# Splitting per-head sums, roots and VectorE's half of the output projection into plan steps of their own, in a two-layer backbone kernel on one core

## What is computed

```
h = modulate(rms_norm(x), shift1, scale1)
q_na, k_na, v_na, p, cq, ckv, krope = split(h @ w_in)     # 384 384 384 256 256 128 32 columns
q_na, k_na = rms_norm per head (6 heads of 64)
q_mla      = rms_norm per head(rms_norm(cq) @ w_uq)        # 6 heads of 96
k_mla, v   = from rms_norm(ckv) @ w_ukv and krope, k normed per head
o = concat(neighbourhood attention, pooling, latent attention)
x = x + gate1 * (o @ w_out)
h2 = modulate(rms_norm(x), shift2, scale2)
x = x + gate2 * peer(h2)   # 8 heads x 16 experts per token: rows u[e], v[e] of 1024 floats, gathered
```

## Time and profile before

| | us |
|---|---|
| three runs, median (lowest to highest) | 4258.71 (4248.27 to 4259.67) |
| the profiled execution's own time | 4255.55 |
| its span in the trace | 4253.7 |
| PE busy in it | 3637.2 (86%) |
| POOL busy | 2586.6 (61%) |
| DVE busy | 2550.2 (60%) |
| ACT busy | 963.9 (23%) |

### The profile page before, as it was taken

One profiled execution on the slowest core, in us unless ns is written; L12 is line 12 of the kernel. 1 busy time (PEld: TensorE's weight loads), 2 busy tenths in 40 slices (PEclk: granted clock), 3 DMA queues, 4 the chain that ended last, 5 costly groups with the idle time before them and its releaser, 6 DMA issues.

```text
span 4253.7 us, 37633 instructions
## 1 busy us (share of the span) xinstructions
PE 3637.2 (86%) x10554; PEld 1695.8 (40%) x10554; DVE 2550.2 (60%) x6442; ACT 963.9 (23%) x2490; POOL 2586.6 (61%) x2833
## 2 busy tenths in 40 slices
PE   7889899989988888888877899999898887777777
PEld 3354454545434223443332355554443432222222
DVE  1165456767665546566666555677676566666663
ACT  1212222222221112122222222222231122122121
POOL 0047446666665556676667663566676677777775
PEclk8899999999999999999999999999999999999999
DMA  6467889999999999999999988999999999999998
GB/s 240 160 237 270 283 325 391 360 392 403 361 366 383 376 383 354 351 362 351 400 396 409 354 291 298 364 369 389 394 407 350 368 401 406 407 406 405 401 402 325
DMA packets 472259, 1519.95 MB, mean 357 GB/s; under 512 B 59980, under 2 KB 78704, under 8 KB 471544
## 3 DMA queue, kind: packets, MB, share of 16 engines
q0 software_dynamic: 368640, 1342.34, 81.8%
q1 hardware_dynamic: 103416, 175.21, 11.6%
HBM read 1511.70 MB, written 5.67 MB: 357 GB/s over the span
## 4 chain that ended last, share of the span: by engine, by line
PE 44%; DMA 27%; POOL 13%; issue 9%; DVE 4%; ACT 2%; SPq 1%; DVEq 0%; ACTq 0%; POOLq 0%
PE expert_sum L2021 23%; DMA expert_rows<-in_peer_v,experts 23%; POOL expert_rows L989 11%; PE work L1780 4%; DMA expert_rows<-in_peer_u,experts 4%; PE work L1754 4%; PE work L1972 3%; PE work L1987 2%; PE work L1916 2%; PE work L1943 2%; PE work L1728 2%; DVE expert_rows L1697 1%; POOL stat_rstd L936 1%; PE work L1961 1%; PE work L1872 1%
## 5 line engine op out<-in xcount | busy, mean ns | idle before, releaser
L2021 PE MATMUL expert_sum<-expert_rows,weight_diagonals 128*128 128x512 f32 x5120 | 2481.8, 615 | 438.0 <-DMA expert_rows<-in_peer_v,experts 404.9
L1697 DVE CUSTOM_DVE_ANT_0 expert_rows<-expert_rows,tokens 128x1024 f32<-128x1024 f32 x1280 | 1556.7, 1216 | 846.1 <-DMA expert_rows<-in_peer_u,experts 832.1
L989 POOL DMA_INDIRECT expert_rows<-in_peer_v,experts x1280 | 1232.4, 963 | 921.6 <-PE expert_sum L2021 716.5
L2021 PEld LDWEIGHTS expert_sum<-expert_rows,weight_diagonals 128*128 128x128 f32 x5120 | 912.1, 193 | 1670.4 <-issue 1356.2
L989 POOL DMA_INDIRECT expert_rows<-in_peer_u,experts x1280 | 1219.5, 953 | 464.5 <-issue 348.4
L1263 ACT ACTIVATE weight_diagonals<-ident,expert_weights 128x128 f32<-128x128 f32 x1280 | 451.0, 392 | 600.6 <-PE expert_sum L2021 368.4
L1780 PE MATMUL work<-weight_ring,h_or_mixed 128*128 128x384 f32 (+3 forms) x800 | 252.7, 470 | 3.9 <-DMA weight_ring<-in_w_in 2.2
L1728 PE MATMUL work<-ident,scratch 128*128 128x128 f32 (+1 forms) x782 | 129.8, 289 | 93.3 <-DVE scratch L1355 35.5
L1780 PEld LDWEIGHTS work<-weight_ring,h_or_mixed 128*128 128x128 f32 x800 | 146.8, 194 | 110.2 <-issue 55.7
L1754 PE MATMUL work<-weight_ring,silu_cond 128*2 128x512 f32 x384 | 175.1, 610 | 12.5 <-DMA weight_ring<-in_w_mod 11.5
L1728 PEld LDWEIGHTS work<-ident,scratch 128*128 128x128 f32 (+1 forms) x782 | 99.0, 145 | 186.7 <-issue 72.5
(11 more groups left out here) (173 smaller groups left out, 2475.0 us busy)
## 6 DMA issues: line engine op xcount, KB each, us to landing
weight_ring<-in_w_mod SPq DMA_DIRECT2D x24, 2048.0 KB, 10.7
weight_ring<-in_w_out SPq DMA_DIRECT2D x16, 2048.0 KB, 19.1
weight_ring<-in_peer_wq SPq DMA_DIRECT2D x16, 2048.0 KB, 9.8
expert_rows<-in_peer_u,experts POOLq DMA_INDIRECT x1280, 7.3
expert_rows<-in_peer_v,experts POOLq DMA_INDIRECT x1280, 7.3
weight_ring<-in_w_in SPq DMA_DIRECT2D x12, 1536.0 KB, 8.0
weight_ring<-in_w_in SPq DMA_DIRECT2D x4, 2048.0 KB, 16.5
weight_ring<-in_t_pool SPq DMA_DIRECT2D x4, 2048.0 KB, 10.8
```

What stands on the lines that cost most here:

```text
L989: g.indirect_dma_start(ring[row % n], None, table, bass.IndirectOffsetOnAxis(ap=idx_st[:, col:col + 1], axis=0),).then_inc(row_in[row % n] ...
L1697: v_.tensor_tensor_reduce(out=u_ring[r % U_RING], in0=u_ring[r % U_RING], in1=tokens[:, :], scale=1.0, scalar=0.0, op0=ALU.mult, op1=ALU.a ...
L2021: ins = t_.matmul(acc[:, hf * 512:(hf + 1) * 512], diags[:, at * P:(at + 1) * P], v_ring[row % V_RING][:, hf * 512:(hf + 1) * 512], start= ...
```

## The change

Two new kinds of step, `hs` (head sums, copies and roots) and `oe` (VectorE's part of the output projection), and a new order of the heads' steps. Per chunk or up-projection, VectorE's sums or copies and GpSimd's two root instructions move from `pr`, `up` and `kv` into `hs`; there are 62 `hs` in the plan. `oe` follows each of the 20 `o`; TensorE's part stays at `o`. ScalarE's part of every step stays with its step, but the steps themselves change places. In `heads_of`, `hs` of a product stands ahead of the next product and `sc` behind it; `cq` and `ck` move from ahead of the next D or E product to behind it, next to `up` and `kp`. `up` costs 1.5 where it cost 2.0, `o` and `oe` 4.4 each where `o` cost 8.8, each `hs` 1.0; the heads of the four sample blocks so cost 165.8 where they cost 142.8, those of layer 1's blocks 0 to 2 113.6 (97.1), those of blocks 3 and 4 92.4 (80.4). No arithmetic is added or taken away. The hunks left out rename what is waited for (`x_updated` counts `oe`, `pool_in_ready` and `rope_keys` count `hs`) and enter the new kinds into the tables of each engine.

```diff
@@ -196,8 +196,9 @@
         return 1.8 * len(TAILS[step[2]])
     if kind == "pd":
         return 7.0 if step[2] else 0.5
-    return {"mrow": 7.0, "nT": 1.8, "tu": 0.7, "ct": 0.7, "cq": 0.4, "up": 2.0, "uT": 1.3, "ck": 0.3, "kp": 1.3,
-            "kT": 1.3, "py": 0.4, "pp": 3.5, "s": 1.0, "pt": 1.0, "pv": 0.6, "ot": 1.8, "o": 8.8}.get(kind, 0.2)
+    return {"mrow": 7.0, "nT": 1.8, "tu": 0.7, "ct": 0.7, "cq": 0.4, "up": 1.5, "uT": 1.3, "ck": 0.3, "kp": 1.3,
+            "kT": 1.3, "py": 0.4, "pp": 3.5, "s": 1.0, "pt": 1.0, "pv": 0.6, "ot": 1.8, "o": 4.4, "oe": 4.4,
+            "hs": 1.0}.get(kind, 0.2)
 
 
 def modulation(l, first, last):
@@ -218,11 +219,12 @@
 
 def heads_of_prompt(l):
     b = 0
-    return [("pr", "A", l, b), ("pr", "B", l, b), ("sc", "A", l, b), ("pr", "C", l, b), ("tu", "A", l, b),
-            ("sc", "B", l, b), ("pr", "D", l, b), ("tu", "B", l, b), ("sc", "D", l, b), ("pr", "E", l, b),
-            ("cq", l, b), ("sc", "E", l, b), ("up", l, b), ("ck", l, b), ("us", l, b), ("kp", l, b), ("uT", l, b),
-            ("kv", l, b), ("pd", l, 0, 0), ("py", l, 0, b), ("ks", l, b), ("pd", l, 0, 1), ("py", l, 1, b),
-            ("kT", l, b)]
+    return [("pr", "A", l, b), ("hs", "A", l, b), ("pr", "B", l, b), ("hs", "B", l, b), ("sc", "A", l, b),
+            ("pr", "C", l, b), ("tu", "A", l, b), ("sc", "B", l, b), ("pr", "D", l, b), ("hs", "D", l, b),
+            ("tu", "B", l, b), ("sc", "D", l, b), ("pr", "E", l, b), ("hs", "E", l, b), ("cq", l, b),
+            ("sc", "E", l, b), ("up", l, b), ("hs", "uq", l, b), ("ck", l, b), ("us", l, b), ("kp", l, b),
+            ("uT", l, b), ("kv", l, b), ("hs", "ukv", l, b), ("pd", l, 0, 0), ("py", l, 0, b), ("ks", l, b),
+            ("pd", l, 0, 1), ("py", l, 1, b), ("kT", l, b)]
 
 
 def heads_of(l, blocks):
@@ -233,29 +235,33 @@
     products = [(ch, l, b) for ch in "AB" for b in blocks]
     slots = []
     for i in range(len(products) + 2):
-        slots += [[("tu", *k) for k in products[i - 2:i - 1] if i >= 2] + [("sc", *k) for k in products[i - 1:i] if i]
-                  + [("pr", *k) for k in products[i:i + 1]]]
+        slots += [[("hs", *k) for k in products[i - 1:i] if i] + [("tu", *k) for k in products[i - 2:i - 1] if i >= 2]
+                  + [("pr", *k) for k in products[i:i + 1]] + [("sc", *k) for k in products[i - 1:i] if i]]
     out = [s for slot in slots[:-2] for s in slot] + [("ct", l)] * last
     ends = slots[-2:]
     later = [("pp", l, b) for b in GROUP[1] if last and pooled_later(l, b)]
     for i in range(n + len(keys) + 2):
         j = i - n
+        out += [("hs", "D", l, b) for b in blocks[i - 1:i] if i]
+        out += [("hs", "E", l, b) for b in blocks[j - 1:j] if j >= 1]
+        out += ends.pop(0) if ends else []
         out += [("us", l, b) for b in blocks[i - 2:i - 1] if i >= 2]
         out += [("ks", l, b) for b in keys[j - 2:j - 1] if j >= 2]
-        out += [("cq", l, b) for b in blocks[i - 1:i] if i]
-        out += [("ck", l, b) for b in keys[j - 1:j] if j >= 1]
-        out += ends.pop(0) if ends else []
         out += [("pr", "D", l, b) for b in blocks[i:i + 1]]
         out += later[j:j + 1] if j >= 0 else []
         out += [("pr", "E", l, b) for b in blocks[j:j + 1] if j >= 0]
+        out += [("sc", "D", l, b) for b in blocks[i - 1:i] if i]
+        out += [("sc", "E", l, b) for b in blocks[j - 1:j] if j >= 1]
+        out += [("uT", l, b) for b in blocks[i - 2:i - 1] if i >= 2]
+        out += [("pr", "C", l, b) for b in blocks[j - 2:j - 1] if j >= 2]
+        out += [("cq", l, b) for b in blocks[i - 1:i] if i]
+        out += [("ck", l, b) for b in keys[j - 1:j] if j >= 1]
+        out += [("kT", l, b) for b in keys[j - 2:j - 1] if j >= 2]
         out += [("up", l, b) for b in blocks[i - 1:i] if i]
         out += [("kp", l, b) for b in keys[j - 1:j] if j >= 1]
-        out += [("sc", "D", l, b) for b in blocks[i:i + 1]]
-        out += [("sc", "E", l, b) for b in blocks[j:j + 1] if j >= 0]
-        out += [("pr", "C", l, b) for b in blocks[j - 2:j - 1] if j >= 2]
-        out += [("uT", l, b) for b in blocks[i - 2:i - 1] if i >= 2]
-        out += [("kT", l, b) for b in keys[j - 2:j - 1] if j >= 2]
         out += [("kv", l, b) for b in keys[j - 1:j] if j >= 1]
+        out += [("hs", "uq", l, b) for b in blocks[i - 1:i] if i]
+        out += [("hs", "ukv", l, b) for b in keys[j - 1:j] if j >= 1]
     return out
 
 
@@ -287,7 +293,7 @@
     out += [("ot", l, blocks[0])]
     for i in range(n + 1):
         if i < n:
-            out += [("o", l, blocks[i], 0), ("o", l, blocks[i], 1)]
+            out += [s for j in range(2) for s in (("o", l, blocks[i], j), ("oe", l, blocks[i], j))]
         if i:
             out += [("nT", "n2", l, blocks[i - 1])]
         if i < n:
@@ -425,7 +431,7 @@
         return [((*step, hf), 1, step) for hf in range(2)]
     if kind == "o":
         l, b, j = step[1:]
-        return [(("g", 0, l, b, j), 1, step), (step, 1, step)]
+        return [(("g", 0, l, b, j), 1, ("oe", l, b, j)), (step, 1, ("oe", l, b, j))]
     if kind == "q":
         return [(step, 1, step)]
     if kind == "fin":
@@ -622,12 +628,12 @@
         stat_turns, qn_turns, sq_turns = [], [], []
         for step in plan:
             kind = step[0]
-            if kind == "nx" or kind == "pr" and step[1] != "C":
+            if kind in ("nx", "hs"):
                 stat_turns += [step[1:]]
+            if kind == "pr" and step[1] != "C":
+                sq_turns += [step[1:]]
             elif kind in ("up", "kv"):
-                stat_turns += [("uq" if kind == "up" else "ukv", *step[1:])]
-            if kind == "pr" and step[1] != "C" or kind in ("up", "kv"):
-                sq_turns += [stat_turns[-1]]
+                sq_turns += [("uq" if kind == "up" else "ukv", *step[1:])]
             if kind == "sc":
                 qn_turns += [step[1:]]
             elif kind in ("us", "kv"):
@@ -939,17 +945,11 @@
             def norm(k, l, b):
                 rstd((k, l, b), 1, 1.0 / D, EPS)
 
-            def project(ch, l, b):
-                if ch != "C":
-                    n, mul, add = {"A": (HEADS, 1.0, DH * EPS), "B": (HEADS, 1.0 / DH, EPS),
-                                   "D": (1, 1.0 / QR, EPS), "E": (1, 1.0 / KVR, EPS)}[ch]
-                    rstd((ch, l, b), n, mul, add)
-
-            def queries_up(l, b):
-                rstd(("uq", l, b), HEADS, 1.0, QK * EPS)
-
-            def keys_up(l, b):
-                rstd(("ukv", l, b), HEADS, 1.0 / QK, EPS)
+            def head_roots(k, l, b):
+                n, mul, add = {"A": (HEADS, 1.0, DH * EPS), "B": (HEADS, 1.0 / DH, EPS), "D": (1, 1.0 / QR, EPS),
+                               "E": (1, 1.0 / KVR, EPS), "uq": (HEADS, 1.0, QK * EPS),
+                               "ukv": (HEADS, 1.0 / QK, EPS)}[k]
+                rstd((k, l, b), n, mul, add)
 
             def rope(key):
 
@@ -1398,15 +1398,17 @@
                 dve.wait_ge(gains_in, 96 * (key[1] + 1))
                 v_.tensor_tensor(view, view, g, ALU.mult).then_inc(gained.sem, 1)
 
-            def project(ch, l, b):
-
-                key = (ch, l, b)
-                if ch in "AB":
+            def sums_of_heads(k, l, b):
+
+                key = (k, l, b)
+                if k in ("A", "B"):
                     head_sums(key, heads(sq[:, 0:WIDTH]))
-                elif ch == "D" and not pooled_later(l, b):
+                elif k in ("uq", "ukv"):
+                    head_sums(key, heads(sq))
+                elif k == "D" and not pooled_later(l, b):
                     dve.wait_ge(*stats.filled(key))
                     v_.tensor_copy(pool_in[:, max(b - 1, 0), :], bank(key)[:, 0:POOL_W]).then_inc(pool_in_ready.sem, 1)
-                elif ch == "E":
+                elif k == "E":
                     dve.wait_ge(*stats.filled(key))
                     if b == 0 and l:
                         dve.wait_ge(latent_out, 32 * l)
@@ -1468,7 +1467,6 @@
                     dve.wait_ge(cached_in, 48 * (l + 1))
                 kr = krope[:, b * ROPE:(b + 1) * ROPE].unsqueeze(1).broadcast_to([P, HEADS, ROPE])
                 v_.tensor_copy(km[:, :, DH:], kr).then_inc(assembled.sem, 1)
-                head_sums(key, heads(sq))
 
             def scale_keys(l, b):
                 key = ("ukv", l, b)
@@ -1546,18 +1544,18 @@
                     dve.wait_ge(x1_in, 16 * (l + 1))
                 elif b and j == 0:
                     dve.wait_ge(xs_in, 48 * (l + 1))
-                if prior(of_o, step):
-                    dve.wait_ge(*x_updated.done(prior(of_o, step)))
+                if prior(of_oe, ("oe", l, b, j)):
+                    dve.wait_ge(*x_updated.done(prior(of_oe, ("oe", l, b, j))))
                 dve.wait_ge(*banks.filled(gkey))
-                dve.wait_ge(*banks.filled(step))
                 v_.tensor_copy(gated, bank(gkey)).then_inc(banks.frees(gkey), 1)
                 dve.wait_ge(*banks.freed(gkey))
```

(3 more changed lines are left out.)

20 lines of the change are left out of this document (9 added, 11 removed).

## The result

| | before | after |
|---|---|---|
| median of 11 runs each, us (lowest to highest) | 4257.34 (4248.27 to 4264.84) | 4264.12 (4257.73 to 4278.37) |
| ratio, 95% interval | | 1.0023 [1.0012, 1.0034] |
| the profiled execution, its span | 4255.55, 4253.7 | 4263.72, 4261.9 |

The forecast was a gain of 22 us; it is a loss of 7 us by the medians, 10 by the ratio. By the interval the change is slower; the size is small. On another chip the same kernel gave 1.0014 [0.9999, 1.0028] (e14), which by itself can't be told from no change.

What follows compares the result with a forecast made beforehand. TensorE bounds layer 0's heads and layer 1's blocks 3 and 4; in blocks 0 to 2 no engine is full. Terms -2.2, -11, -6.3, -2, about -22 us: 4233.6, as median 4236.8 us; range 4207 to 4266.

Steps and rivals of the forecast that it cites:

- item 6: Prompt's heads, steps sliding by up to 7 rows, later bias transfers, longer-held product banks: counted at nothing.
- Item 1: Layer 1's blocks 0 to 2: GpSimd no longer waits for the root before gathering, 1.25 us per product; -8 us taken.
- Item 2: TensorE's waits for scaled D go: -6.3, -3, -4.2 us by stretch; in layer 0 also 3.1 and 2.0 us.
- item 3: Waits newly exposed in the heads: `up` 3.7 us (layer 0) and 0.9 (blocks 3 and 4), keys 0.5, `uT` 6.
- Item 4: Last keys' transposes wait less for VectorE: -1 us in layer 0, -3 us in layer 1's blocks 3 and 4.
- Item 5: Output projection: VectorE's 20 waits for the product, nearly all free time; 0.1 us each, -2 us.
- hidden anyway: Rival: GpSimd's root work only delays other gathers, item 1 gives 0 to 2 us; 4250 us; chance 0.29.
- the queries' transposes come too late: Rival: `up`, root, `us`, `uT` have one product between them, exposing query blocks; slower, most likely 4270 us; chance 0.14.

Runs made afterwards that it cites:

- e14: The change itself, unaltered, run again on another chip with slower transfers: 1.0014 [0.9999, 1.0028] of the kernel before, 4456.25 us.
- e4: Kernel before, order of steps untouched, only the heads' costs raised by as much as the change raises them: 1.0026 of the kernel before.
- e1: The changed kernel with the old costs (`hs` 0, `up` 2.0): 0.9981 of the kernel before, 4255.09 us against 4257.66.
- e6: The changed kernel with the old costs (`hs` 0, `up` 2.0) in layer 1's blocks 3 and 4 alone: 1.0004 of the kernel before.
- e9: The changed kernel, new costs kept, with the attention steps of sample block 1 at 1.6 times their cost: 0.9971 of the kernel before.
- e2: The kernel before with only the output projection split into `o` and `oe`, 4.4 each: 0.9991 of the kernel before.
- e5: The changed kernel with old costs and `oe` directly behind `o`, leaving only the new order: 0.9975, 4243.54 us against 4255.28 before.
- e8: The changed kernel with old costs and `uT` moved behind the next `cq` or `up`: 0.9989 of the kernel before.
- e11: Old costs, `oe` at `o`, the new order only for the A and B products: 0.9965 of the kernel before.
- e12: Old costs, `oe` at `o`, the new order only for D, E and the up-projections, A and B as before: 1.0001 of the kernel before.

## Why the prediction was wrong

**The step that failed is item 6, "at nothing"**: "Steps that keep their engine time but slide by up to 7 rows change only what they run beside". What they run beside is what covers their waits. The slide cost 14.1 us in rows 664 to 734 in the change and 14.5 in e4. e4 (the slide alone, 1.0026) and e1 (all but the slide, 0.9981) show it from both sides, e6 with its repair in that stretch and e9 with another one. The text counted how many of the first 92 rows the heads would take (61 for 58) and did not look at which steps a row would fall between. The trace of the kernel before had the price, 1.46 us per latent head with one row for two, in its own layer 0.

**Item 1** (-8 us): right in its mechanism, too large in the end. The wait for the root went, TensorE's row became the next limit as said, and the gap from product to gather shrank by 1.10 us where 1.25 was counted. The sign named for it failed: the first period stayed at 1659.36 - 1641.13 = 18.23 us and didn't fall to 17 (six rows in both kernels; later ones hold seven rows for six and can't be compared). At equal costs, from the first A product's start to the last D product's, 53 rows, the kernel before and e2 took 169.8 and 173.2 us, and with the new order e1, e5 and e8 took 164.2, 160.1 and 165.4: some 8 us, the size of the item. But over rows 408 to 592 the first two took 570.8 and 575.3 us, the three others 572.9, 568.2 and 572.3: some 2 us were left, less than these profiles can tell. On the chip of e11 and e12 more was left, 578.6 us with the new order of A and B against 588.7 without. Of the 6.1 us that the change shows in rows 408 to 450, e4 shows 3.7 without the new order, because fewer steps fall there. Why the rows behind the D products give back part of it was not tried.

**Item 2** (-6.3, -3, -4.2 and -5.1): the waits for scaled D went or fell to 0.9 us in all stretches, and so did the 2.0 us of L1850, but the 3.1 us before the A transposes of layer 0 rose to 4.4. e12, in which the waits for D go as well, is worth nothing within its interval; **item 3** is a likely reason, as what it exposes is of the same size. Its sizes were good: `up` waited 4.0 us (3.7 said), `uT` 4.51 and 4.47 (3 each said, up to 5.6 allowed). With the 4.4 us before the A transposes that makes 13.6 us of L974 and L1399 in layer 0 besides the last keys, more than the 10 us that the prediction had named as a sign of being wrong.

**Item 4**: in layer 0 the last keys waited 8.82 us instead of 7.33 (-1 was said), in layer 1 8.3 fell to 2.8 (-5.5, where -3 was said).

**Item 5** (-2): e2 gives -4 [-9, +2] us, which holds it and also zero.

The order by itself was to bring about 20 us (the sum without item 5); e5 shows 11. The rival "hidden anyway" gave the order 5 to 11 us, but from the wrong items: it put item 1 at 0 to 2 us and kept the items 2 to 5, while e11 (A and B alone, 4418.37 us) against e12 (all the rest, 4434.70) says the reverse. Its time (4250) was not reached because of the slide. The rival "the queries' transposes come too late" lies nearest to the measured time (4270), but not by its mechanism: e1 and e5 have those waits (6.4 us for rope in each) and are faster than the kernel before, and e4, which has the old order, is slower. That GpSimd's gathers would suffer from a freed VectorE didn't come: 976 and 953 ns after, 986 and 951 before.

Still open: the kernel before started row 0 at 245.9 us, all the others between 237.0 and 243.5 us, e2 and e4 with the same prompt's heads among them (238.1, 240.0). Its granted clock was lower there, 0.71 over 160 to 246 us where the change had 0.79. e4 has the same plan up to row 0, had 0.78 and started it at 240.0, so this is scatter. So most of the 7 us that after seems to gain ahead of row 0 isn't the change's, and the profile-to-profile sum (+8.2) understates the loss in the stages (+15). The medians, +7 to +10, stand between the two.

## What to carry to other kernels

In an order fixed when the program is built, a cost is not an estimate of time alone: it decides which piece of filler stands between a step and the step that needs its result. After each change of costs or order, list for every chain over two engines (scores to transposes, norm to transposes) how many pieces of filler lie between its ends, and compare the lists before and after. A gain found in one stage can be taken back by a stage that the change never names; test the order and the costs apart, as e4 and e5 do. And compare stages only between edges that no step crosses.
